# A two-stage block on one core: the experts' products with the wait for a weight tile's low part in the middle of the tile

## What is computed

```python
def hier_moe(h, w_rg, b_rg, w_re, b_re, w_gate, w_up, w_down):
    ...
    comb = (g_oh[..., None] * e_w[..., None, :]).astype(h.dtype)
    out = jnp.zeros_like(h)
    for g in range(N_GROUPS):
        hid = jax.nn.silu(jnp.einsum("bld,edf->blef", h, w_gate[g])) * jnp.einsum("bld,edf->blef", h, w_up[g])
        out = out + jnp.einsum("blef,ble,efd->bld", hid, comb[:, :, g], w_down[g])
    return out
```

## Time and profile before

| | us |
|---|---|
| median of 3 runs | 1451.03 |
| lowest and highest | 1450.0 and 1451.44 |
| the profiled execution | 1451.07 |
| its span, first to last instruction | 1449.3 |
| PE busy in the span | 1335.0 (92%) |
| DVE busy | 850.7 (59%) |
| ACT busy | 726.7 (50%) |
| POOL busy | 612.0 (42%) |
| L306, L307, L308 in the experts' stage, products each | 256 |

### The profile page before, as it was taken

The page is one execution under the profiler, slowest core; times in us unless marked ns, Lnnn a source line. Parts: engine busy times, 40 slices in busy tenths (PEclk is TensorE's granted clock), DMA queues, the critical chain, the costliest instruction groups (busy, mean ns, idle before and its releaser), DMA issues.

```text
span 1449.3 us, 22617 instructions
## 1 busy us (share of the span) xinstructions
PE 1335.0 (92%) x7921; PEld 1073.5 (74%) x7921; DVE 850.7 (59%) x1447; ACT 726.7 (50%) x1233; POOL 612.0 (42%) x324
## 2 busy tenths in 40 slices
PE   7989998887899999999668999999999998999997
PEld 6877877676677787877546777776788876788886
DVE  1482344334688888888646889984777765210112
ACT  5555455333476666757553334556433333543443
POOL 5858667531000000000165656756300005778785
PEclk9989998589899999999988999899999999999999
DMA  7736444016489999999437546544200005455562
GB/s 225 197 112 186 139 136 139 0 58 188 158 292 327 301 329 308 331 317 299 135 108 201 153 129 189 155 134 144 89 2 2 3 16 160 154 160 186 168 197 92
DMA packets 129094, 239.94 MB, mean 166 GB/s; under 512 B 17072, under 2 KB 34298, under 8 KB 129008
## 3 DMA queue, kind: packets, MB, share of 16 engines
q1 hardware_dynamic: 116656, 227.12, 49.6%
q10 hardware_dynamic: 12353, 11.66, 3.1%
HBM read 234.56 MB, written 1.05 MB: 163 GB/s over the span
## 4 chain that ended last, share of the span: by engine, by line
PE 47%; issue 36%; POOL 7%; DVE 7%; ACT 3%; DMA 0%; ACTq 0%; POOLq 0%; SPq 0%; DVEq 0%
PE bank L320 7%; PE bank L324 7%; PE bank L321 7%; POOL wlo L300 7%; DVE work L814 2%; PE bank L3057 2%; PE bank L3055 2%; PE bank L3056 2%; PE bank L2405 2%; PE bank L2419 2%; PE bank L2424 1%; PE bank L2381 1%; PE bank L391 1%; PE bank L1987 1%; PE bank L306 1%
## 5 line engine op out<-in xcount | busy, mean ns | idle before, releaser
L300 POOL TENSOR_TENSOR wlo<-raw,whi 128x1024 fp32r<-128x1024 f32 (+1 forms) x232 | 570.5, 2480 | 671.5 <-ACT whi L295 666.9
L295 ACT ACTIVATE whi<-raw 128x1024 fp32r<-128x1024 f32 (+1 forms) x300 | 309.0, 1052 | 249.2 <-PE bank L324 180.7
L320 PE MATMUL bank<-whi,t0h 128*128 128x512 f32 (+1 forms) x632 | 258.2, 409 | 4.9 <-ACT whi L295 2.7
L321 PE MATMUL bank<-whi,t0l 128*128 128x512 f32 (+1 forms) x632 | 252.6, 400 | 0.0
L324 PE MATMUL bank<-wlo,t0h 128*128 128x512 f32 (+1 forms) x632 | 173.8, 397 | 0.5 <-POOL wlo L300 0.5
L320 PEld LDWEIGHTS bank<-whi,t0h 128*128 128x128 f32 x632 | 122.9, 194 | 37.8 <-ACT whi L295 4.6
L321 PEld LDWEIGHTS bank<-whi,t0l 128*128 128x128 f32 x632 | 122.1, 193 | 27.1 <-issue 1.0
L324 PEld LDWEIGHTS bank<-wlo,t0h 128*128 128x128 f32 x632 | 120.4, 191 | 29.0 <-POOL wlo L300 1.6
L306 PE MATMUL bank<-whi,t0h 128*128 128x512 f32 x296 | 124.0, 419 | 7.1 <-DVE wlo L300 4.5
L308 PE MATMUL bank<-whi,t0l 128*128 128x512 f32 x296 | 118.1, 399 | 0.0
L307 PE MATMUL bank<-wlo,t0h 128*128 128x512 f32 x296 | 117.8, 398 | 0.0
(11 more groups left out here) (484 smaller groups left out, 2421.8 us busy)
## 6 DMA issues: line engine op xcount, KB each, us to landing
raw<-in_w_ff SPq DMA_DIRECT2D x64, 512.0 KB, 3.8
raw<-in_w_in SPq DMA_DIRECT2D x60, 496.0 KB, 3.5
raw<-in_w_in SPq DMA_DIRECT2D x56, 512.0 KB, 3.7
work<-in_w_exp_down SPq DMA_DIRECT2D x68, 256.0 KB, 6.3
work<-in_w_exp_gate SPq DMA_DIRECT2D x62, 256.0 KB, 5.7
work<-in_w_exp_up SPq DMA_DIRECT2D x62, 256.0 KB, 6.9
raw<-in_w_exp_down SPq DMA_DIRECT2D x60, 256.0 KB, 5.5
raw<-in_w_exp_gate SPq DMA_DIRECT2D x34, 256.0 KB, 5.9
```

The costliest lines, as they stand in the source:

```text
L295: nc.scalar.activation(whi[:, s, 0:width], raw_of(n)[:, 0:width], ACT.Copy).then_inc(hi_ready, 1)
L300: ins = (nc.vector if split_by_vector(n) else nc.gpsimd).tensor_tensor(wlo[:, s, 0:width], raw_of(n)[:, 0:width], whi[:, s, 0:width].bitca ...
L320: nc.tensor.matmul(dst[t][:, 0:width], hi[:, k, r], wh[:, kk, :], start=k == 0 and not begun, stop=False)
L321: nc.tensor.matmul(dst[t][:, 0:width], lo[:, k, r], wh[:, kk, :], start=False, stop=False)
```

## The change

In `gate_up` and in `down` PE waits for the tile's high part (`hi_ready`) ahead of the first product. The four products with the weights' high part come first, then stands the wait for the low part, then the two products with the weights' low part. A tile keeps its six products, its banks and its signal `quarter_done` on the last one. DVE, ACT, SP and POOL keep their programs.

```diff
--- before.py
+++ after.py
@@ -1480,14 +1480,19 @@
 
                 if q == 0:
                     pe.wait_ge(hid_ready, E + 1)
-                wait_low(pe, n, u, per)
+                pe.wait_ge(hi_ready, n + 1 + per * u)
                 s = n % RING
                 wh, wl = (w[:, s, :].rearrange("p (a k n) -> p a k n", a=2, k=2) for w in (whi, wlo))
                 dst = bank[e_par][:, :].rearrange("p (a n) -> p a n", a=2)
                 r = slice(par * P, (par + 1) * P)
                 for kk in range(2):
                     k = 2 * q + kk
-                    mm = times(dst, t0h[:, k, r], t0l[:, k, r], wh[:, :, kk, :], wl[:, :, kk, :], k == 0, k == KC - 1)
+                    nc.tensor.matmul(dst, t0h[:, k, r], wh[:, :, kk, :], start=k == 0, stop=False)
+                    nc.tensor.matmul(dst, t0l[:, k, r], wh[:, :, kk, :], start=False, stop=False)
+                wait_low(pe, n, u, per)
+                for kk in range(2):
+                    k = 2 * q + kk
+                    mm = nc.tensor.matmul(dst, t0h[:, k, r], wl[:, :, kk, :], start=False, stop=k == KC - 1)
                 mm.then_inc(quarter_done, 1)
 
             def turn_hidden(E, e_par):
@@ -1500,14 +1505,16 @@
             def down(n, c, E, e_par, u, per, first=False, last=False):
                 if c == 0:
                     pe.wait_ge(hid_low, E + 1)
-                wait_low(pe, n, u, per)
+                pe.wait_ge(hi_ready, n + 1 + per * u)
                 s = n % RING
+                hh, hl = t1h[:, 2 * e_par + c, 0:P], t1l[:, 2 * e_par + c, 0:P]
                 for h in range(2):
                     f = slice(512 * h, 512 * h + 512)
-                    hh, hl = t1h[:, 2 * e_par + c, 0:P], t1l[:, 2 * e_par + c, 0:P]
                     nc.tensor.matmul(bank[4 + h][:, :], hh, whi[:, s, f], start=first, stop=False, skip_group_check=True)
-                    nc.tensor.matmul(bank[4 + h][:, :], hh, wlo[:, s, f], start=False, stop=False, skip_group_check=True)
-                    mm = nc.tensor.matmul(bank[4 + h][:, :], hl, whi[:, s, f], start=False, stop=last,
+                    nc.tensor.matmul(bank[4 + h][:, :], hl, whi[:, s, f], start=False, stop=False, skip_group_check=True)
+                wait_low(pe, n, u, per)
+                for h in range(2):
+                    mm = nc.tensor.matmul(bank[4 + h][:, :], hh, wlo[:, s, 512 * h:512 * h + 512], start=False, stop=last,
                                           skip_group_check=True)
                 mm.then_inc(quarter_done, 1)
```

## The result

| | before | with the change |
|---|---|---|
| runs | 6 | 6 |
| median, us | 1451.24 | 1441.18 |
| lowest and highest, us | 1449.19 and 1456.89 | 1437.66 and 1444.01 |
| span of the profiled execution, us | 1449.3 | 1442.2 |

The ratio of the changed kernel to the one before is 0.9914, 95% interval 0.9891 to 0.9937: 12.5 us less, with 9 to 16 us as bounds. The forecast was 8.2 us less, 1442.9, with a range from 1440.0. The median lies inside that range; the ratio times the 1451.03 us from which the forecast was made is 1438.6, which lies outside. Timed twice more, the same kernel gave 0.9934 (0.9908 to 0.9960) and 0.9931 (0.9913 to 0.9950).

A forecast was written before the change was run, and what follows sets the result against it. The prediction took TensorE (PE), working 92% of the span, as the bound. Terms of 3.3 + 1.0 + 2.9 + 1.0 = 8.2 us off 1451.07 us gave 1442.9 us, range 1440.0 to 1446.4.

The forecast's parts named there:

- first down tiles: Each expert's first down tile: PE's late start behind the last gate product goes, 22 x 0.15 = 3.3 us.
- expert 0: PE's 2.22 us idle for expert 1's low part: four products run inside it, 0.93 us, 1.0 with the weight load.
- three turns with their nine tiles: Turns between groups: the head start covers PE's idle time, limited to DVE's 0.98 us each, 2.9 us with nine first down tiles.
- expert 31: Last expert, no gate tiles to cover the chain: PE starts on the high part, 0.93 + 0.08 = 1.0 us gained.
- the scatter's wait: PE's wait for DVE's addition L1566 at the scatters: not shorter but longer, 1.2 to 1.4 us each.
- The added waits: A second wait at 192 tiles: costed at 0, covered by PE's product spacing; other end 21 us.
- The loads: Expert weights, 3.15 MB each: the needed 365 GB/s can follow, since transfers moved 391 GB/s and SP waited for slots.
- A: First down tiles: the small gaps stay, not being the low part's; 4.9 us remain, 1446.2; chance 0.09.
- B: Inside a group the loads become the limit; the same 4.9 us, 1446.2; chance 0.03.
- C: PE's own queue pays for the second wait at 192 tiles; 21 us cost at 0.11 each, 1463.9; chance 0.03.
- D: The change doesn't do what it says, high part as late as low, or DVE sets the pace; about 1449; chance 0.03.
- Nothing behind the stretch is changed: Behind the experts' products: no change counted, and the stretch's effect on PE's clock taken as before.

The follow-up runs named there:

- experiment 4: The changed kernel, but the low part again waited for ahead of each tile's first product, order and second wait kept; ratio 1.0000 (0.9981 to 1.0018).
- experiment 2: The changed kernel with the head start for down tiles alone, gate tiles waiting for their low part first; ratio 0.9938 (0.9915 to 0.9961).
- experiments 5: The changed kernel with two products instead of four ahead of the wait for the low part; one run of 1445.74 us, stretch 313.77 us.
- experiment 6: The changed kernel, with DVE making the scatter's first addition between the second and third low part, not behind the fourth; ratio 0.9887 (0.9857 to 0.9917).

## Why the prediction was right about the stretch and wrong about what lies behind it

**The sum over the stretch** held: 8.2 us forecast, 8.92 measured. Term by term, from scatter to scatter and at the ends:

| term | forecast, us | shown by |
|---|---|---|
| first down tiles, 0.15 each | 3.3 | 31 spacings of 0.46 or 0.47 for two products; 3.5 us, what the other terms leave |
| expert 0 | 1.0 | idle time 2.22 to 1.19, 1.03 |
| three turns with their nine tiles | 2.9 | 3 x 1.14 = 3.4 |
| expert 31 | 1.0 | from its transposition (702.27, now 690.94) to the scatter (709.84, now 697.51) 7.57 to 6.57: 1.00 |

A group takes 79.69 - 77.80 = 1.89 us less from scatter to scatter; less five first down tiles at 0.15 that is 1.14 us for a turn, where I had 0.98. The mechanism at the turn was right: DVE has no idle time left ahead of L1624, and the scatter's wait grew to 1.28 us (forecast 1.2 to 1.4). DVE's own rows say the same: from the gathered rows' low part (L1474) to the scatter's first addition it took 23.60 to 23.62 us and now takes 22.51, 1.1 less. Its two idle times gave about 0.5 each, and 0.1 came from a place that I had not listed, the low part behind L1617 at 480.76, which started 0.43 us after it and with the change 0.33:

```profile
480.76 0.41 DVE L1617 TENSOR_TENSOR t1l<-bank,t1h 128x256 fp32r<-128x256 f32 x1
481.19 2.36 DVE L300 TENSOR_TENSOR wlo<-work,whi 128x1024 fp32r<-128x1024 f32 x2
```

```profile
474.32 0.42 DVE L1624 TENSOR_TENSOR t1l<-bank,t1h 128x256 fp32r<-128x256 f32 x1
474.65 2.35 DVE L300 TENSOR_TENSOR wlo<-work,whi 128x1024 fp32r<-128x1024 f32 x2
```

This is the mis-sized term, 0.4 to 0.5 of the 0.7 us. The rest is in the first down tiles: I read a late start of 0.36 to 0.38 us as a loss of 0.15, but the product behind it was late too, as here at expert 0:

```profile
407.19 0.40 PE L308 MATMUL bank<-whi,t0l 128*128 128x512 f32 x1
407.57 0.47 PE L1508 MATMUL bank<-whi,t1h 128*128 128x512 f32 x1
407.88 0.39 PE L1509 MATMUL bank<-wlo,t1h 128*128 128x512 f32 x1
```

That is 0.38 + 0.31 us for two spacings of 0.233, 0.22 lost. Of the 22 tiles in the term, six are of this kind.

**The added waits** at 0: right, by experiment 4. **The loads**: right. SP still waits 110.5 us for slots, ACT isn't idle for a transfer in the stretch, and the experts take 8.63 us instead of 8.77. At 3.15 MB each that is 365 GB/s, more than the 358 GB/s that the Trainium skill, "DMA: Bandwidth & Descriptors", section Specifications, gives per core; the trace doesn't agree with that as a limit for a core that runs alone. **Rivals** A, B, C and D are all out: A by experiment 2, B by the stretch, C by experiment 4, D by the stretch as well. What came true was none of them: a gain behind the stretch.

**The step that failed** is the sentence "Nothing behind the stretch is changed; what it does with PE's clock I take as before", together with the range built on it. The instructions behind the stretch are the same, but PE's clock was not: the same 58 products ran at a granted clock of 1.00 in 14.2 us, where the kernel before had 0.81 and 17.6, and 146 us behind the scatter the changed kernel was 2.4 us further ahead, in all its three profiles. With the stretch's 8.92 that is 11.4 us at this point, against a forecast of 8.2. From there on the executions of one program differ among themselves by more than that, so the profiles don't say how much of the 2.4 us is left at the end.

The second fault is the size of the scatter. I took 1451.03 us, the median of three runs that lay within 1.5 us, for the level of the kernel before. Over 52 runs its times go from 1447.1 to 1458.9, and the means of its four groups of runs are 1452.3 to 1453.0. The low end of the range, 1440.0, held my doubts about the head start and nothing for this scatter of some 3 us per run (the piece above alone varies by 7 us with the clock). The first comparison came out at 12.5 us with an interval that reaches 9.1; the two others at 9.6 and 10.0. The 19 runs of the changed kernel have a mean of 1442.4, the 52 of the kernel before 1452.8: 10.4 us less, with 9 to 12 as bounds (two standard errors). So the change is worth about 10 us, 8.9 in the stretch and one or two behind it, and the last two of the 12.5 are most simply chance.

## What to carry to other kernels

Where an engine waits for two parts of an operand, wait for each ahead of its first reader: four products of head start took 1 us off each long wait and all of each short one, and the second wait cost nothing. Then ask which engine's chain runs behind the gain: here DVE's kept a third of a microsecond per group; changing its order too, and ACT's at one end, was worth another 6 us. And size a stage between two landmarks of the trace: that repeated within 0.1 us where whole runs scattered by 3. Then set the same landmarks behind the stage: a change in one stage moved PE's clock in another, 90 us later, and 2.4 us came of it that a sum over the stage alone can't have.

## What the runs showed of the hardware

- The granted clock falls in some executions of an unchanged program and not in others, at the same place: 60.3 us became 67.7 for the same work.
- At another place, some 90 us behind the experts' products, it falls or not by how these are written: 0.81 in all five profiles without the head start in the down tiles, 1.00 in all seven with it, 17.6 against 14.2 us for the same 58 products.
- A fall can also come behind short idle times: in experiments 5 and 6 the last tile of expert 31 ran at 0.43 us per product, behind a wait of 1.5 us and a shorter one. Three profiles of the changed kernel have the same two waits as experiment 6 and kept 0.23 us, so the waits alone don't decide it.
